# Mixer A's probabilities turned by VectorE and GpSimd instead of TensorE, in a float32 hybrid attention layer

## The reference

```python
h = rms_norm(x, pre_norm_w[l]);  proj = h @ w_in[l]             # 256 x 4096 by 4096 x 14384
oa = nsa_mixer(...)                                             # mixer A, three gated branches
o_cmp = p_cmp @ vc                                              # compressed keys
o_slc = softmax(mask(q_rot @ ks)) @ vs                          # all 4 blocks are selected at SEQ = 256
o_win = softmax(causal(q_rot @ kw)) @ vw                        # window of 512, so plainly causal
o = gates[..., 0:1] * o_cmp + gates[..., 1:2] * o_slc + gates[..., 2:3] * o_win
mix = concat([oa * silu(za), ob * silu(zb)]);  x = x + rms_norm(mix @ w_out[l], post_norm_w[l])
```

## Time and profile before

| | us |
|---|---|
| median of three runs | 1790.21 |
| the profiled execution | 1790.47 |
| its span, first to last instruction | 1788.5 |
| TensorE busy | 1782.3 |
| VectorE busy | 1130.3 |
| ScalarE busy | 882.0 |
| GpSimd busy | 259.2 |

### The profile page before, as it was taken

How to read it: one execution, slowest core, us unless ns; L and a number is a source line. 1 busy time by engine, 2 the same in 40 slices (tenths; PEclk the granted TensorE clock), 3 DMA queues, 4 the chain that set the end, 5 groups by cost and what they waited for, 6 DMA issues and landing times.

```text
span 1788.5 us, 22716 instructions
## 1 busy us (share of the span) xinstructions
PE 1782.3 (100%) x8102; PEld 1476.1 (83%) x8102; DVE 1130.3 (63%) x1190; ACT 882.0 (49%) x1200; POOL 259.2 (14%) x250
## 2 busy tenths in 40 slices
PE   9999999999999999999999999999999999999998
PEld 7888888888888888888888888888888888888886
DVE  7656656787877868655575557555755684444445
ACT  7643455464545445356445643564456554444443
POOL 2330003102121030430033103310331000000000
PEclk9999999999999999999999999999999999999999
DMA  8866677656555565666666656666666666667665
GB/s 293 254 195 188 189 232 226 177 155 176 152 173 162 159 176 155 183 192 190 171 192 193 194 166 191 197 189 175 189 190 194 182 190 219 208 206 211 214 203 206
DMA packets 184264, 344.76 MB, mean 193 GB/s; under 512 B 15216, under 2 KB 19568, under 8 KB 184176
## 3 DMA queue, kind: packets, MB, share of 16 engines
q1 hardware_dynamic: 183456, 342.58, 65.6%
q10 hardware_dynamic: 720, 0.93, 0.1%
HBM read 339.27 MB, written 4.19 MB: 192 GB/s over the span
## 4 chain that ended last, share of the span: by engine, by line
PE 99%; DMA 0%; ACT 0%; SPq 0%; DVE 0%; ACTq 0%; issue 0%
PE acc L570 31%; PE acc L576 31%; PE acc L573 31%; PE acc L801 1%; PE trans L587 1%; PE trans L706 1%; PE scores L790 0%; PE scores L647 0%; DMA raw<-in_w_in 0%; PE scores L691 0%; PE scores L689 0%; PE scores L690 0%; PE heads L725 0%; PE heads L724 0%; PE heads L723 0%; PE scores L599 0%
## 5 line engine op out<-in xcount | busy, mean ns | idle before, releaser
L1221 DVE TENSOR_TENSOR w_parts<-raw,w_parts 128x1024 fp32r<-128x1024 f32 x620 | 782.4, 1263 | 579.2 <-ACT w_parts L909 577.9
L909 ACT ACTIVATE w_parts<-raw 128x1024 fp32r<-128x1024 f32 x620 | 656.6, 1059 | 662.6 <-PE acc L576 649.8
L570 PE MATMUL acc<-w_parts,x_parts 128*128 128x512 f32 x2424 | 950.9, 392 | 0.3 <-DVE w_parts L1221 0.3
L576 PE MATMUL acc<-w_parts,x_parts 128*128 128x512 f32 x2424 | 944.5, 390 | 0.0
L573 PE MATMUL acc<-w_parts,x_parts 128*128 128x512 f32 x2424 | 943.6, 389 | 0.0
L576 PEld LDWEIGHTS acc<-w_parts,x_parts 128*128 128x128 f32 x2424 | 455.0, 188 | 96.4
L573 PEld LDWEIGHTS acc<-w_parts,x_parts 128*128 128x128 f32 x2424 | 455.4, 188 | 92.2
L570 PEld LDWEIGHTS acc<-w_parts,x_parts 128*128 128x128 f32 x2424 | 455.3, 188 | 92.1 <-issue 0.7
L519 POOL COPY rot<-tok_b 32x256 f32<-32x256 f32 x112 | 76.1, 680 | 566.9 <-DVE tok_b L1570 562.6
L481 POOL TENSOR_TENSOR rot<-tok_a,trig 128x512 f32<-128x512 f32 x18 | 30.6, 1699 | 358.2 <-ACT tok_a L1004 188.2
L1560 DVE RECIPROCAL mixed<-mixed 128x256 f32<-128x256 f32 x32 | 55.9, 1748 | 0.5
(11 more groups left out here) (233 smaller groups left out, 816.0 us busy)
## 6 DMA issues: line engine op xcount, KB each, us to landing
raw<-in_w_in SPq DMA_DIRECT2D x478, 512.0 KB, 3.7
raw<-in_w_out SPq DMA_DIRECT2D x128, 512.0 KB, 4.3
raw<-in_w SPq DMA_DIRECT2D x16, 512.0 KB, 4.6
x_tok<-in_x SPq DMA_DIRECT2D x16, 256.0 KB, 5.1
xt_raw<-in_x_t SPq DMA_DIRECT2D x7, 512.0 KB, 5.7
wpost<-in_post_w SPq DMA_DIRECT2D x8, 256.0 KB, 4.9
out<-y SPq DMA_DIRECT2D x3, 512.0 KB, 2.8
out<-y SPq DMA_DIRECT2D x5, 256.0 KB, 2.1
```

Of the source, the lines that this page charges most:

```text
L570: nc.tensor.matmul(o, stat_hi, mov_hi, start=(k == 0), stop=False)
L576: last = nc.tensor.matmul(o, stat_lo, mov_hi, start=False, stop=(k == KB - 1))
L909: nc.scalar.activation(w_hi[:, n % SPLIT_SLOTS, :, 0:width], raw[:, n % RAW_SLOTS, :, 0:width], ACT.Copy).then_inc(hi_ready, 1)
L1221: V.tensor_tensor(w_lo[:, s, :, 0:width], raw[:, n % RAW_SLOTS, :, 0:width], w_hi[:, s, :, 0:width].bitcast(F32), ALU.subtract).then_inc(l ...
```

## The change

TensorE's six turns of a group are gone. VectorE transposes the probabilities in 32x32 blocks, in place, two units at a time (`turn_pair`, a 128x1024 transpose, three a group), and GpSimd moves the blocks (`move_probs_a`): tile 0's into `rot` with 16 copies of 32x256, tile 1's with 32 copies of 32x128 for units 2 and 3 and 32 more for units 4 and 5, into `qraw_t` and `tok_a`, which are free then. The high and low parts are made from these tiles in SBUF rather than from PSUM. Units 2 to 5 are no longer multiplied by VectorE: ScalarE does it with two scaled copies of 128x256 a unit. The steps move: turns 0 and 1 from 10, 11 to 13, 14 and their values from 11, 12 to 14, 15; turns 2 to 5 from steps 1 to 4 of the mixing chunk to 7 to 10, their values from 2 to 5 to 8 to 11.

```diff
-FILLS_A = 9
+FILLS_A = 3
...
-TURN_STEPS = {10: 0, 11: 1}
-VALUE_STEPS = {11: 0, 12: 1}
-LATE_TURN_STEPS = {1: 2, 2: 3, 3: 4, 4: 5}
-LATE_VALUE_STEPS = {2: 2, 3: 3, 4: 4, 5: 5}
+TURN_STEPS = {13: 0, 14: 1}
+VALUE_STEPS = {14: 0, 15: 1}
+LATE_TURN_STEPS = {7: 2, 8: 3, 9: 4, 10: 5}
+LATE_VALUE_STEPS = {8: 2, 9: 3, 10: 4, 11: 5}
...
+            def move_blocks(src, dst):
+                for i in range(QUARTERS * QUARTERS):
+                    rows, cols = [slice(v * QUARTER, (v + 1) * QUARTER) for v in divmod(i, QUARTERS)]
+                    last = nc.gpsimd.tensor_copy(dst[cols, :, :, rows], src[rows, :, :, cols])
+                return last
...
+            def move_probs_a(g):
+                pool.wait_ge(probs_turned, 3 * g + 1)
+                move_blocks(probs[:, 0:2, :].rearrange("p u (j r k) -> p r (u j) k", j=2, r=2),
+                            rot[:, :, :].rearrange("p r (h q) -> p r h q", h=HPG)).then_inc(probs_moved, 1)
+                for i, units in enumerate((probs[:, 2:4, :], probs_more[:, :, :])):
+                    pool.wait_ge(probs_turned, 3 * g + 2 + i)
+                    for r in range(2):
+                        last = move_blocks(units.rearrange("p u (r b k) -> p r b u k", r=2, b=TILES)[:, r, :, :, :],
+                                           turned_late[r][:, :, 2 * i:2 * i + 2, :])
+                    last.then_inc(probs_moved, 1)
...
+            for g in range(GROUPS):
                 rotate_a(g)
+                move_probs_a(g)
                 move_mixed(g)
...
-                if n in TURN_STEPS:
-                    turn_a(TURN_STEPS[n], unit, fill)
...
             def values_a(u, g):
                 t, branch, b = TURNS_A[u]
-                pe.wait_ge(tr_free, fill + 4 + u)
+                pe.wait_ge(pt_ready, 6 * g + u + 1)
...
-            def first_turned(u, fill):
-                act.wait_ge(tr_done, fill + 4 + u)
-                nc.scalar.activation(pt_hi[:, u % 2, :], trans[:, :], ACT.Copy).then_inc(pt_hi_ready, 1)
+            def first_turned(u, g):
+                act.wait_ge(probs_moved, 3 * g + (1 if u < 2 else 3))
+                if u > 1:
+                    act.wait_ge(values_done, 4 * g + u - 1)
+                nc.scalar.activation(pt_hi[:, u % 2, :], turned_a[u], ACT.Copy).then_inc(pt_hi_ready, 1)
...
+                    if at - 1 in UNIT_STEPS and UNIT_TILES_A[UNIT_STEPS[at - 1]]:
+                        u = UNIT_STEPS[at - 1]
+                        act.wait_ge(weight_done, 6 * g + u + 1)
+                        for i in range(2):
+                            p = unit_probs[u][:, i * SEQ:(i + 1) * SEQ]
+                            last = nc.scalar.activation(p, p, ACT.Copy, scale=weight[:, u % 4, i:i + 1])
+                        last.then_inc(probs_ready, 1)
...
-                V.tensor_tensor(pt_lo[:, u % 2, :], trans[:, :], pt_hi[:, u % 2, :].bitcast(F32), ALU.subtract
-                                ).then_inc(tr_free, 1)
+                V.tensor_tensor(pt_lo[:, u % 2, :], turned_a[u], pt_hi[:, u % 2, :].bitcast(F32), ALU.subtract
+                                ).then_inc(pt_ready, 1)
+
+            def turn_pair(u, unit):
+                pair = probs[:, u - 1:u + 1, :] if u < 5 else probs_more[:, :, :]
+                dve.wait_ge(probs_ready, unit + u + 2)
+                V.transpose(pair, pair).then_inc(probs_turned, 1)
...
+                        if u == 1:
+                            turn_pair(u, unit)
+                    if at - 2 in UNIT_STEPS and UNIT_STEPS[at - 2] == 3:
+                        turn_pair(3, unit)
...
+                    if of_a and n == LEAD:
+                        turn_pair(5, UNITS_A * group)
```

More of the change, by code:

```diff
@@ L211, in build @@
         norm_w, _ = sb("norm_w", [P, KB])
+        turned_late = [t[:, :, :].rearrange("p a n -> p (a n)").rearrange("p (b h q) -> p b h q", b=TILES, h=HPG)
+                       for t in (qraw_t, tok_a)]
+        turned_a = [rot[:, r, :] for r in range(2)] + [turned_late[r][:, b, :, :].rearrange("p h q -> p (h q)")
+                                                       for r in range(2) for b in range(TILES)]
         assert at[0] <= nc.sbuf_usable_end, at[0]
@@ L315, in build @@
         v_ready = sem("v_ready")
+        probs_turned = sem("probs_turned")
+        probs_moved = sem("probs_moved")
+        values_done = sem("values_done")
         pt_hi_ready = sem("pt_hi_ready")
+        pt_ready = sem("pt_ready")
         b_turned = sem("b_turned")
@@ L516, in move_mixed @@
                 dst = rot[:, :, :].rearrange("p i (h q) -> p (i h) q", q=SEQ)
[L517 to L521, removed]
+                last = move_blocks(tok_b[:, :, :].rearrange("p t (h d) -> p t h d", h=HPG),
+                                   dst.rearrange("p h (t q) -> p t h q", t=TILES))
                 last.then_inc(mix_moved, 1)
                 pool.wait_ge(heads_taken, TILES * (group + 1))
-            rotate_a(0)
-            move_mixed(0)
-            for g in range(1, GROUPS):
+            def move_probs_a(g):
[9 more added lines that the diff above has]
+            for g in range(GROUPS):
                 rotate_a(g)
+                move_probs_a(g)
                 move_mixed(g)
@@ L692, in scores_a, with rest_of_a, values_a @@
                 last.then_inc(scores_done, 1)
-            def turn_a(u, unit, fill):
+            def rest_of_a(n, g):
+                if n in LATE_VALUE_STEPS:
+                    values_a(LATE_VALUE_STEPS[n], g)
+            def values_a(u, g):
                 t, branch, b = TURNS_A[u]
[L697 to L718, removed]
-                pe.wait_ge(tr_free, fill + 4 + u)
+                pe.wait_ge(pt_ready, 6 * g + u + 1)
                 stat_hi = v_hi[:, branch, b, g * P:(g + 1) * P]
@@ L726, in values_a @@
                                         skip_group_check=True)
+                if u < 4:
+                    last.then_inc(values_done, 1)
                 if u == 5:
@@ L857, in _ @@
                 for n in range(PAIRS):
-                    rest_of_a(n, g, UNITS_A * g, FILL_A + per * g)
+                    rest_of_a(n, g)
                     gemm_pair(C_A + 1 + 2 * g, n, 0)
@@ L863, in _ @@
                     if g == 0:
-                        rest_of_a(n, GROUPS - 1, UNIT_B - UNITS_A, FILL_B - FILLS_A)
+                        rest_of_a(n, GROUPS - 1)
                     gemm_pair(C_B + 4 * g, n, 0)
@@ L1061, in attention_a_frame @@
                     if at in TURN_STEPS:
-                        first_turned(TURN_STEPS[at], fill)
+                        first_turned(TURN_STEPS[at], g)
                     split(c, n)
@@ L1144, in _ @@
                 attention_a_frame(C_A + 2 * g, g, FILL_A + per * g, UNITS_A * g)
[L1145 removed]
+                mixing_frame(C_A + 1 + 2 * g, 2 * g, g)
             attention_a_frame(C_B - 1, GROUPS - 1, FILL_B - FILLS_A, UNIT_B - UNITS_A)
[L1147 removed]
+            mixing_frame(C_B, 2 * (GROUPS - 1), GROUPS - 1)
             with act.Fori(0, GROUPS - 1) as g:
@@ L1454, in mask_unit, with normalise_unit @@
                 V.tensor_reduce(negmax[:, slot % 4, 0:nh], p, AX.X, ALU.max, negate=True).then_inc(max_ready, 1)
-            def normalise_unit(t, nh, slot, unit, recips, weights=None, gate=None):
+            def normalise_unit(t, nh, slot, unit, recips, weights=None, gate=None, whole=True):
                 nk = P * (t + 1)
@@ L1469, in normalise_unit @@
                     f = weight[:, slot, 0:nh]
+                    if not whole:
+                        return
                     dve.wait_ge(weight_done, weights + 1)
@@ L1544, in attention_a_frame @@
                         gate = gates[:, t, bass.ds(HPG * g + (u - 2 if t else 2 * u), 1 if t else 2), 1:3]
-                        normalise_unit(t, 2 if t else 4, u, unit + 1 + u, 6 * g + u, 6 * g + u, gate)
+                        normalise_unit(t, 2 if t else 4, u, unit + 1 + u, 6 * g + u, 6 * g + u, gate, t == 0)
+                        if u == 1:
+                            turn_pair(u, unit)
+                    if at - 2 in UNIT_STEPS and UNIT_STEPS[at - 2] == 3:
+                        turn_pair(3, unit)
             def mix_tile(at, group):
```

4 lines of the change are left out of this document (1 added, 3 removed).

## The result

The changed kernel takes **1801.16 us** (median; 1800.07 to 1803.33), the kernel before 1790.26 (1790.13 to 1791.10): the ratio is 1.0061, interval 1.0049 to 1.0074. It is slower by 10.9 us; the forecast was 1796 in a range of 1780 to 1812. The profiled execution took 1800.79 us, its span 1799.0.

A forecast was written before the change was run, and what follows sets the result against it. TensorE, busy 1782.3 of 1788.5 us, was taken to bound the kernel. Waits of 3.5 and 0.9 us in four groups less 11.5 for the turns gave +6.1, so 1796 us, in a range of 1780 to 1812.

The forecast's parts named there:

- The turns: TensorE's queue: removing 24 turns of four transposes saves 0.48 us each, 11.5 us in all.
- The price of a small copy: GpSimd's 32x128 copies: 0.28 us each, 0.32 from start to start, between bounds of 0.197 and 0.394.
- Rival (c): GpSimd's small copies cost as much as large ones, 0.394 us: 1825 us; chance 0.11, shared with another rival.
- GpSimd's first move: Attention chunk, tile 0: 16 copies of 32x256 with three splits among them, from 33.5 to 43.4 us.
- The two late moves: GpSimd, tile 1: 64 small copies without pause from 45.4, 20.5 us plus 9.8 for ten splits, ending at 77.6.
- The last small term, 1.9: Late moves: two low parts, two gate multiplications and two of L1556 hold GpSimd's copies up about 1.9 us.
- TensorE at value 2: Mixing chunk's first value, step 8: TensorE arrives at 75.5, operand at 79.0, so 3.5 us of waiting in four groups.
- Value 0: Attention chunk's first value, step 14: TensorE arrives at 45.4 and waits 0.9 us, the low part standing behind VectorE's transpose.
- No second wait, the old 16 copies in time: Mixing chunk: ScalarE's splits ready by 80.5, needed at 86.5; GpSimd's old 16 copies end by 91.
- Rival (d): Each 3.5 us TensorE wait lowers the clock, 10 us on top of the forecast, 1806 us; chance 0.09.
- rival (a): GpSimd's copies done before mixing step 8, only the attention chunk's first value waits: 1782.3 us, at best 1778.7; chance 0.27.
- the prediction's term of 0.9 us for the low parts: VectorE's low parts, reading two SBUF tiles, shut GpSimd out; otherwise the copies end 0.9 us earlier and sum is +2.5.

The follow-up runs named there:

- two-steps kernel: Changed kernel with turns 2 to 5 at mixing-chunk steps 9 to 12 and their values at 10 to 13, two steps later: 1782.22 us.
- the kernel with the low part ahead: two-steps kernel with VectorE's transpose of units 2 and 3 put behind tile 0's first low part: 1788.52 us.
- best version: two-steps kernel with turns 0 and 1 and their values one step later, and turns 2 to 5 and theirs one step later too: 1779.14 us.
- the filler kernel: Changed kernel with twelve idle 128x512 matmuls ahead of value 2 in each group, result unread: 1795.35 us.
- the kernel in which VectorE scales: Changed kernel with units 2 to 5 multiplied by VectorE again and ScalarE's scaled copies removed: 1811.53 us.
- the kernel one step later: Changed kernel with turns 2 to 5 at mixing-chunk steps 8 to 11 and their values at 9 to 12: 1790.40 us.
- one-copy kernel: Changed kernel with one GpSimd copy instead of sixteen in each of a group's five sets, so turned probabilities are incomplete: 1780.51 us.

## Why the prediction was right, and what it left out of its sum

The times below are from the start of the attention chunk, 448.67, predicted against measured in group 1.

- **The turns**, 0.48 a turn: 0.41, 0.43 and 0.473 by three ways of measuring, 11.5 against 9.8 to 11.4. Right, and closest to the measurement without any lateness in it.
- **The price of a small copy**, 0.28: the least is 0.283, the median 0.288. Rival (c), the same cost as the large one, is refuted. It was the widest open term, and the two-input operations of the same engine bounded it well.
- **GpSimd's first move**: begins 33.5 against 33.7, ends 43.4 against 44.4. Sixteen copies took 10.71 us rather than 9.9. Of the miss of 1.0, 0.2 is a later start. The other 0.8 is one more block of VectorE: three splits were counted, but a fourth was under way when the move began, and its first copy took 1.23 us.
- **The two late moves**: 64 copies with their blocks 32.2 against 32.3 (493.57 to 525.89); end 77.6 against 77.2. Ten splits were forecast and ten held a copy. The last small term, 1.9, is 2.1 by the forecast's own prices (twice 0.44, 0.43 and 0.17) and took 1.8. The operand at value 2: 79.0 against 78.7.
- **TensorE at value 2**: 75.5 against 75.4. The wait: 3.5 against 3.37, 3.33, 3.33 and 3.68. The two-steps kernel shows that the loss was this wait and the clock behind it.
- **Value 0**: TensorE is there at 45.4 as predicted, the wait was put at 0.9 and is 0.48. The step gave as its reason that the low part stands behind the transpose of units 2 and 3; that is false. The end of the first move, 1.0 later than worked out, sets it, as the kernel with the low part ahead shows. The value taken came within 0.4 by the wrong road, and the error helped the sum by luck (below).
- **No second wait, the old 16 copies in time**: right; they end at 88.6 against 91.
- **The clock** is the term that was missing. The forecast priced each wait at its length, and put the fall of the clock into rival (d) with a chance of 0.09. It happened behind three waits of four. Half a clock in such a stretch costs about 1.6 us (104.93 and 105.02 against 103.35). Rival (d) had the mechanism, but a size of 10 us where three falls cost 4.9. Its price came from a misreading. The matmuls of 622 ns at the start say nothing of a fallen clock, for the granted clock was 1.00 there (kernel before, the first 6 us, columns as above):

```profile
0.00:6.00 6.00, 4.78 (x11) 3.87 (x12) 1.11 (x4) 2.87 (x5) 0.20 (x4) 1.00 0.71 219
```

- **The restart** behind a wait is a second term put at nothing. The changed kernel's third group waits 3.79 us by the distances (3.33 and 0.46), but is 4.2 longer than a group of the best version: 0.4 a group.

By these sizes: the third group, without a fall, is 103.35, and 99.14 without any wait, so the waits with their restarts cost 4.2 a group (4.4 predicted). 4 x 4.2 - 11.4 + 3 x 1.6 = +10.2, against 10.5 in the spans. Had the clock stayed up, the result would have been about 1795.4, the filler kernel's time, and the forecast was 1796. That this comes so close is in part luck: value 0's wait was put 0.4 too high, and the restart of 0.4 that was left out hides it.

What remains open is why the clock did not fall behind the third group's wait, which was as long as the first two. The falls don't keep a fixed distance from the waits. In the changed kernel they begin 0.4, 1.2 and 1.4 us after the wait's end. In the kernel in which VectorE scales two begin 1.0 us before it, and these are the two that last twice as long.

The break-even named for rival (a) was 2.9 us of waiting a group. The profiled execution of the kernel one step later waited 8.7 us in all by the distances, 2.2 a group, and its span was 1.1 shorter than before. So the true break-even is 2.4 to 2.5. The turns were priced right; the difference of 0.4 is again the restart.

The chain shows what such a fall looks like to a reader. It is the changed kernel's chain in group 1 (start, us, what), against the earlier trace rows:

```profile
525.60 0.30 POOL tok_a L526
526.00 0.64 ACT pt_hi L1047
526.66 0.70 DVE pt_lo L1491
527.41 0.50 PE heads L726
...
528.39 0.24 PE acc L592
528.93 0.43 PE acc L598
...
532.27 0.23 PE acc L595
```

Four engines hand over in 1.8 us, then the matmuls go from 0.24 to 0.43 and back.

## What to carry to other kernels

Work moved off the busiest engine pays what it cost there only if its results are placed as late as the new chain needs: work out the end of that chain in the consumer's steps and put the consumer a step behind it, since each microsecond of waiting is paid in full. To a wait of TensorE add its restart, 0.4 us a group here, and for one of some 3 us the fall of the clock that can follow it, 1.6 us here. Look at the granted clock behind every such wait, since the page counts that loss as busy time. When the placing is one table of numbers, try the neighbours; here three steps for tile 1's values and one for tile 0's turned 0.6% slower into 0.6% faster.

## What the runs showed of the hardware

- **The clock.** Waits of 3.33 to 3.68 us in a running stream brought 3.4 us at 1.2 GHz in three cases of four. Waits of 4.13 to 4.45 did so in four of four, twice for 6.8 us. Behind waits of 1.72 to 2.04 and all shorter ones, in seven kernels, no trace shows a fall; the untraced executions of the kernel one step later leave this in doubt for 1.72 to 2.04. With twelve idle matmuls in the wait the clock stayed at 2.4 GHz.
- **Which VectorE operations shut GpSimd out.** These are the moved blocks' copies in the changed kernel's trace that began inside a VectorE operation. All were held inside a split (two SBUF inputs, 76 of 76), a low part (24 of 24) and a gate multiplication (8 of 8). Also held were the 8 of 8 that began inside L1581, an addition of a constant with one SBUF input and SBUF output: 0.386 to 0.390 us instead of 0.283. None was held inside block transposes (35), maxima (22), masks with one input in PSUM (19) and scaled copies out of PSUM (9), or in 72 of 80 cases inside a reciprocal; the other 8 copies began right ahead of a split and were held by it. This settles the prediction's term of 0.9 us for the low parts: the Trainium skill (SBUF — State Buffer, "SBUF: two separate sides") names two SBUF inputs, and a two-port mode, as the cases in which VectorE takes the port pair alone, and the low parts, which read two SBUF tiles now, do so. One form is an exception here: inside L1481, with two SBUF inputs but only 128x2 elements, 8 of 8 copies went undisturbed.
- **The lock works both ways.** In the one-copy kernel VectorE's low part takes 0.69 us alone and 0.88 when it begins during a copy. A split takes 1.23 alone and, in the changed kernel, up to 1.46 when it begins during a copy.
- **A small GpSimd copy** of 32x128 is 0.283 us, one of 32x256 0.390: by these two sizes 0.176 is fixed and 0.107 goes with 128 elements.
